# Two banks for the output products of four attention stages, a two-scalar scaling on GpSimd, and the compressed branch moved into the first units

## The reference, cut to what matters

```
o_c = softmax(where(valid_c, q kc^T * scale, NEG_BIG)) * valid_c @ vc      # 31 compressed keys
o_s = softmax(causal(q ks^T * scale)) @ vs
o_w = softmax(causal(q kw^T * scale)) @ vw
o_n = g0 * o_c + g1 * o_s + g2 * o_w
```

## Time and profile before

| | |
|---|---|
| median of 3 runs | 3747.55 (3745.74 to 3749.96) |
| the profiled execution's own time | 3756.65 |
| its span | 3754.8 |
| TensorE busy, share of the span | 3329.8 (89%) |
| VectorE, ScalarE, GpSimd busy | 1294.7, 976.5, 401.7 |
| mean granted TensorE clock | 0.943 |
| stage "at", layer 0 | from 261.2 to about 418 |
| stage "at", layer 1 | from 1148.0 to about 1310 |
| stage "mla" | from 2085.6 to about 2156 |
| stage "gqa" | from 2962.4 to about 3081 |

### The profile page before, as it was taken

How to read it: one execution, slowest core, us unless ns; L and a number is a source line. 1 busy time by engine, 2 the same in 40 slices (tenths; PEclk the granted TensorE clock), 3 DMA queues, 4 the chain that set the end, 5 groups by cost and what they waited for, 6 DMA issues and landing times. The chain is left out here.

```text
span 3754.8 us, 42733 instructions
## 1 busy us (share of the span) xinstructions
PE 3329.8 (89%) x17174; PEld 2288.9 (61%) x17174; DVE 1294.7 (34%) x1709; ACT 976.5 (26%) x1557; POOL 401.7 (11%) x403
## 2 busy tenths in 40 slices
PE   7999899998999899999756769999988787999996
PEld 6875587877876487787644367444436346644442
DVE  4324543333523444242344543111113644311112
ACT  4225333222324414231221431000013343100001
POOL 1005100000104300000000610000000561000000
PEclk9999999999998999999977989999998898999998
DMA  5410223333320014331300123999982101499996
GB/s 154 124 45 1 68 81 99 90 90 80 106 90 23 12 56 135 90 93 42 101 7 14 45 80 120 416 424 424 424 341 80 45 23 58 195 420 424 424 423 289
DMA packets 286517, 587.41 MB, mean 156 GB/s; under 512 B 34666, under 2 KB 228408, under 8 KB 237200
## 3 DMA queue, kind: packets, MB, share of 16 engines
q1 hardware_dynamic: 286352, 585.11, 41.9%
HBM read 581.92 MB, written 2.10 MB: 156 GB/s over the span
## 5 line engine op out<-in xcount | busy, mean ns | idle before, releaser
L2010 PE MATMUL ps<-w_ring,xe 128*64 128x512 f32 x1024 | 232.7, 597 | 6.7 <-PEq L109 5.0
L305 PE MATMUL ps<-h_hi,in_w_hi 128*128 128x512 f32 (+1 forms) x528 | 210.1, 398 | 12.8 <-DVE in_w_lo L353 8.2
L305 PE MATMUL ps<-u_hi,mlp_w_hi 128*128 128x512 f32 x512 | 202.3, 395 | 12.0 <-DVE u_lo L976 12.0
L305 PE MATMUL ps<-h_lo,in_w_hi 128*128 128x512 f32 (+1 forms) x528 | 208.4, 395 | 0.0
L305 PE MATMUL ps<-h_hi,in_w_lo 128*128 128x512 f32 (+1 forms) x528 | 207.8, 394 | 0.0
L353 DVE TENSOR_TENSOR mlp_w_lo<-w_ring,mlp_w_hi 128x2048 fp32r<-128x2048 f32 x64 | 146.7, 2292 | 176.9 <-ACT mlp_w_hi L321 176.9
L305 PE MATMUL ps<-h_hi,mlp_w_hi 128*128 128x512 f32 x512 | 199.3, 389 | 3.0 <-DVE h_lo L367 3.0
L305 PE MATMUL ps<-u_lo,mlp_w_hi 128*128 128x512 f32 x512 | 201.4, 393 | 0.0
L305 PE MATMUL ps<-u_hi,mlp_w_lo 128*128 128x512 f32 x512 | 201.1, 393 | 0.0
L305 PE MATMUL ps<-h_lo,mlp_w_hi 128*128 128x512 f32 x512 | 199.2, 389 | 0.0
L305 PE MATMUL ps<-h_hi,mlp_w_lo 128*128 128x512 f32 x512 | 199.2, 389 | 0.0
(11 more groups left out here) (513 smaller groups left out, 7176.0 us busy)
## 6 DMA issues: line engine op xcount, KB each, us to landing
w_ring<-in_w SPq DMA_DIRECT2D x192, 1024.0 KB, 12.8
ex_front<-in_w SPq DMA_DIRECT2D x96, 1024.0 KB, 13.3
ex_back<-in_w SPq DMA_DIRECT2D x96, 1024.0 KB, 13.5
w_ring<-in_w_in SPq DMA_DIRECT2D x32, 1024.0 KB, 6.4
w_ring<-in_w_up SPq DMA_DIRECT2D x32, 1024.0 KB, 5.8
w_ring<-in_w_down SPq DMA_DIRECT2D x32, 1024.0 KB, 5.7
w_ring<-in_cmp_w SPq DMA_DIRECT2D x16, 512.0 KB, 4.2
w_ring<-in_w_out SPq DMA_DIRECT2D x8, 1024.0 KB, 6.4
```

What stands on the lines that cost most here:

```text
L305: mm = pe.matmul(ps[0:o.rows, k % banks, 0:o.cols], lhsT, rhs, start=(j == 0), stop=(j == len(o.mm) - 1))
L2010: mm = pe.matmul(ps[rows, bank + half, :], lhsT, slot(2 * m + a)[:, kk, 512 * half:512 * half + 512], start=(k == 0), stop=(k == DC - 1))
```

## The change

It has three parts.

1. The output products of successive chunks alternate between banks 6 and 7 (`bank_of`). The first product of a chunk now waits for the `o_done` of the chunk before last.
2. GpSimd scales the probabilities of ungated groups with two scalars, the second a column of ones, in place of one.
3. In "at", only the two mask products stay ahead of the first unit. `cmp_scores` moves to step 2. The VectorE maxima and subtraction follow in step 2, ScalarE's exponential in step 3, VectorE's sums in step 4, GpSimd's multiplication before its unit 4, and `cmp_flip` with its two copies in step 6; it now uses banks 6 and 7 and not T_BANK. The wait for `sel` moves into the first unit, the wait for the copies to the first output product.

```diff
+C_SCORES, C_FLIP = 2, LAG + TT - 1
...
+    def bank_of(g):
+        return O_BANK + (chunks_done[g] - closes(g)) % 2
...
+                    if cmp and u == 0:
+                        pe.wait_ge(s.sel_made, 1)
...
-                    elif cmp:
-                        pe.wait_ge(s.c_copied, 2)
...
-                        if opens and chunks_done[g] - closes(g) > 0:
-
-                            pe.wait_ge(s.o_done, chunks_done[g] - closes(g))
+                        if cmp and g == 0:
+
+                            pe.wait_ge(s.c_copied, 2)
+                        if opens and chunks_done[g] - closes(g) > 1:
+
+                            pe.wait_ge(s.o_done, chunks_done[g] - closes(g) - 1)
...
-                    cmp_scores()
-                    pe.wait_ge(s.sel_made, 1)
+                    cmp_masks()
                 for step in range(nu + LAG + 1 + TT):
+                    if cmp and step == C_SCORES:
+                        cmp_scores()
                     if step < nu:
                         scores(step)
-                    if cmp and step == LAG - 1:
+                    if cmp and step == C_FLIP:
                         cmp_flip()
...
                 for u in range(nu):
+                    if cmp and u == C_SCORES + 2:
+                        pool.wait_ge(s.c_inverse, 1)
...
-                        if groups[g].gate:
-                            ins = pool.tensor_scalar(p, p, inv[:, u % 8, a:a + 1], groups[g].gate(a, i), ALU.mult, ALU.mult)
-                        else:
-                            ins = pool.tensor_scalar(p, p, inv[:, u % 8, a:a + 1], None, ALU.mult)
+                        gate = groups[g].gate(a, i) if groups[g].gate else C.ones[:, 0:1]
+                        ins = pool.tensor_scalar(p, p, inv[:, u % 8, a:a + 1], gate, ALU.mult, ALU.mult)
```

More of the change, by code:

```diff
@@ L706, in keep @@
                         act.wait_ge(s.mixed, mixed_by[g])
-                        act.activation(oT.hi[:, groups[g].chunk, :], ps[:, O_BANK, :], ACT.Copy).then_inc(s.o_hi, 1)
+                        act.activation(oT.hi[:, groups[g].chunk, :], ps[:, bank_of(g), :], ACT.Copy).then_inc(s.o_hi, 1)
                 for step in range(nu + LAG + 2 + TT):
-                    if cmp and step == 0:
+                    if cmp and step == C_SCORES + 1:
                         act.wait_ge(s.c_less, 1)
@@ L716, in _ @@
                         exponentials(step)
-                    if cmp and step == LAG - 1:
+                    if cmp and step == C_FLIP:
                         act.wait_ge(s.c_flipped, 1)
-                        act.activation(pcT[:, 0, :], ps[:, T_BANK, :], ACT.Copy).then_inc(s.c_copied, 1)
+                        act.activation(pcT[:, 0, :], ps[:, 6, :], ACT.Copy).then_inc(s.c_copied, 1)
                     if 0 <= step - LAG < nu:
@@ L771, in keep @@
                         dve.wait_ge(s.o_hi, chunks_done[g])
-                        dve.tensor_tensor(oT.lo[:, c, :], ps[:, O_BANK, :], oT.hi[:, c, :].bitcast(F32), ALU.subtract).then_inc(s.o_done, 1)
+                        dve.tensor_tensor(oT.lo[:, c, :], ps[:, bank_of(g), :], oT.hi[:, c, :].bitcast(F32), ALU.subtract).then_inc(s.o_done, 1)
                 v = pc[:, :, :, :, :].rearrange("p a i r n -> p (a i r) n") if cmp else None
@@ L777, in _ @@
                                           C.ident[:, LO:LO + H1].unsqueeze(2).broadcast_to([P, H1, P]), ALU.add).then_inc(s.sel_made, 1)
+                    u = step - LAG - 2 - (TT - 1)
+                    if u >= 0 and u % TT == TT - 1:
+                        keep(u // TT)
+                    if step < nu:
+                        peaks(step)
+                    if 1 <= step <= nu:
+                        inverses(step - 1)
+                    if cmp and step == C_SCORES:
                         dve.wait_ge(s.c_scored, 1)
@@ L782, in _ @@
                         dve.tensor_tensor(v, c_ps, c_small[:, 0, :].unsqueeze(2).broadcast_to([P, 32, 32]), ALU.subtract).then_inc(s.c_less, 1)
-                    u = step - LAG - 2 - (TT - 1)
-                    if u >= 0 and u % TT == TT - 1:
-                        keep(u // TT)
-                    if step < nu:
-                        peaks(step)
-                    if cmp and step == 1:
+                    if cmp and step == C_SCORES + 2:
                         dve.wait_ge(s.c_exped, 1)
@@ L797, in _ @@
                         ins.then_inc(s.c_inverse, 1)
-                    if 1 <= step <= nu:
-                        inverses(step - 1)
-                    if cmp and step == LAG - 1:
+                    if cmp and step == C_FLIP:
                         dve.wait_ge(s.c_flipped, 2)
-                        dve.tensor_copy(pcT[:, 1, :], ps[:, T_BANK + 1, :]).then_inc(s.c_copied, 1)
+                        dve.tensor_copy(pcT[:, 1, :], ps[:, 7, :]).then_inc(s.c_copied, 1)
                     if 0 <= step - LAG < nu:
```

18 lines of the change are left out of this document (8 added, 10 removed).

## The result

The changed kernel takes 3711.44 us (median of 4 runs, 3706.27 to 3716.81). The kernel before, measured in the same session, takes 3748.09. The difference of the medians is 36.65 us where 28.3 were forecast. The ratio on record is 0.9891 with a 95% interval of 0.9874 to 0.9908. In all measurements here this ratio is not the plain quotient of the two medians (0.9902 in this one), so it should be read with its interval. 3711.4 lies inside the forecast range (3706 to 3735), on its fast side. The profiled execution took 3716.81 us with a span of 3715.0 and a mean granted clock of 0.947; before, the span was 3754.8 and the clock 0.943. One run of a later kernel, `split_012`, took 4390.28 us at a granted clock of 0.728: it is in that kernel's median (without it 3709.09), but not in its ratio.

A forecast was written before the change was run, and what follows sets the result against it. TensorE was taken to be held at chunk openings by the output bank's wait, with clock falls behind them. Gains of 16.3 + 0.6 + 5.4 + 6.0 = 28.3 us took the median 3747.55 to 3719.2 us, range 3706 to 3735.

The forecast's parts named there:

- What bounds the stages: Four attention stages: TensorE stops at chunk openings for the output bank; GpSimd's equally long 3.09 us "gqa" round isn't the bound.
- Part 1: Chunk openings: two output banks remove TensorE's wait, 10.4 us in "at", 4.6 in "gqa", 1.3 in "mla", 16.3 in all.
- The lower bound of half: Two output banks: gain of only 8 us if earlier openings merely lead to waits for exponentials two units later.
- Part 2: GpSimd scaling with two scalars: mostly cover, saving 0.6 us where flips wait for GpSimd alone; bounds 0 and 3.
- The walk through layer 1: Start of "at", layer 1, traced engine by engine: first output product at 1176.6 instead of 1179.06, 2.4 us earlier.
- Part 3: Compressed branch moved at the starts of "at": 2.4 us in layer 1, 3.0 in layer 0, 5.4 in all; bounds 0 and 8.
- I take the middle: Start of "at", layer 0: 3.0 us, between 1.8 (clock falls at the same time) and 4.2 (full units keep it up).
- The rival of a branch stretched over units without room: "at", steps 2 to 4: VectorE's extra 4.6 us gives back half the openings' gain; 15 us, 3733; chance 0.12.
- Part 4: Clock falls behind openings vanish once the idle goes: 6 us taken, between 1.8 and 10.9, since the profiled execution exceeded the median.
- The clock that still falls behind the 32-row products: Sparse openings of "at": clock still falls though the idle is gone; gain 22.3 us, 3725; chance 0.25.
- the one that falls behind all eight: Sparse openings: denser narrow work makes the clock fall behind all eight, 37 us lost instead of 10.9; 3751; chance 0.03.
- GpSimd as the pace of "gqa": "gqa" rounds: GpSimd sets the 3.09 us, hiding shape changes that could be shorter; 16 us more, 3703; chance 0.04.

The follow-up runs named there:

- split_012: The changed kernel with the 64 narrow products issued in three pieces, in steps 0, 1 and 2: 3713.83 us, ratio 0.9881.
- scalars_only: The kernel before with only the two-scalar scaling on GpSimd: 3753.49 us, ratio 0.9999.
- banks_only: The kernel before with only the two alternating output banks and their wait: 3722.78 us, ratio 0.9913.
- one_scalar: The changed kernel with GpSimd's one-scalar scaling of before, keeping the two banks and the moved branch: 3726.91 us, ratio 0.9937.
- after_again: The changed kernel run once more, with nothing changed, in a later session: 3713.8 us, ratio 0.9892.
- branch_only: The kernel before with only the compressed branch moved (one output bank, one scalar): 3737.2 us, ratio 0.9965.
- old_wait: The changed kernel, banks still alternating, but waiting for the split of the chunk just before: 3737.11 us, ratio 0.9948.
- scores_1: The changed kernel with the narrow products in step 1 instead of step 2: 3721.91 us, ratio 0.992.
- scores_3: The changed kernel with the narrow products in step 3 instead of step 2: 3729.51 us, ratio 0.9934.
- old_wait_no_pieces: The changed kernel with the old wait at openings and without the 32-row products, leaving out the compressed attention's share of the output: 3724.87 us, single run.

## Why the prediction held, and where its steps were off

**What bounds the stages** held in the main. TensorE's round of 3.09 us in "gqa" is there with GpSimd at half its work (`scalars_only`). The prediction was wrong, though, that 0.17 us is the only idle on the load side: the round also has 0.76 and 0.81 us there, the latter put down to GpSimd's product in the kernel before. It is 0.81 us in `scalars_only` too, now without GpSimd as its releaser, and the matmuls show no idle beside it in either kernel, so it held nothing up. And the openings did wait for the bank and for nothing else.

**Part 1**: 16.3 us forecast, 17.6 measured between the profiles. By stage 10.4, 4.6 and 1.3 were forecast and 11.2, 4.9 and 1.5 found. The "at" part was counted by its waits, and there each opening gives some 0.07 us more than its wait. An opening in "gqa" was said to shorten by 0.67 and shortened by 0.71. The lower bound of half, for later waits on exponentials, did not come up: no such wait stands in the openings. By the case in the Trainium skill ("TensorE: Matmul & The Clock Gate", HAM oscillation) in which double-buffering gave no further gain, this part would have been 0; `banks_only` gave 29.7 us with the clock's share, so the case does not carry over to banks that TensorE is seen to wait for.

**Part 2**: 0.6 us forecast, and alone it is within its bounds of 0 and 3 (ratio 0.9999). In "mla" and "gqa" it gave 0.9 where 0.6 was said. What was mis-sized is the share that was put inside part 3, "a similar 0.6 per layer": `one_scalar` shows 2.08 us in layer 0, and 3.7 in layer 1 against a start with the same clock. The walk through layer 1 took GpSimd as free when the branch's sums were ready, which is true with two scalars and false with one.

**Part 3**: 5.4 us forecast, 2.5 measured between the two profiles: 2.7 in layer 1 against 2.4, and nothing (-0.2) in layer 0 against 3.0. The step that failed is the choice in layer 0 between a clock that falls at the same time (1.8) and one that two full units keep up (4.2), "I take the middle". It was neither: the clock fell 0.9 us after the first product, at 261.4 and not at 265.2, and the narrow products took 7.04 us. The walk in layer 1 was good in its result (28.6 said, 28.36 found) and in its last wait (0.4 said, 0.38 found). Since the start depends on when the clock falls, single profiles are poor evidence, so here is the time to the first output product in all profiles of the four arrangements, sorted by the time from the start of the stage to the clock's fall:

| | narrow products first, fall within 1.2 us | the same, fall at 3.0 to 4.0 us | step 2, fall within 1.2 us | step 2, fall at 6.2 to 7.3 us |
|---|---|---|---|---|
| one scalar | 31.03, 31.37, 31.34 | 28.17, 29.36, 28.14 | 30.43, 30.44 | 27.67, 27.69 |
| two scalars | 31.00, 31.01 | none | 28.35, 28.36, 28.38, 28.35, 28.36, 28.35 | 23.96, 24.95 |

With a fall within 1.2 us, parts 2 and 3 together give 2.7 to 3.0 us a layer, 5.4 to 6 in both, where 5.4 were forecast; part 3 with one scalar gives only 0.6 to 0.9. In the pair of profiles layer 0 compares a late fall before (28.17) with an early one after (28.35), and that hides half of it. Which of the two a layer gets is luck. The rival of a branch stretched over units without room did not happen with step 2, and does happen with 1 and 3.

**Part 4**, the clock, was mis-sized: 6 us were taken, 12.4 measured. Two things are in that. The falls behind openings were worth 10.8 in the profile, as read (10.9), but a fall at the end of "gqa" (5.30 against 3.65 us for 16 products) was not seen at all, though it stood in the timeline. No 32-row product is near it, only 2.0 us of idle. It is the most regular fall of all: the 16 products take 5.25 to 5.35 us in all six profiles with the old wait, and 3.65, behind an idle of 1.36, in all eight without it. So the theory that a fall wants both the idle and the product holds for idles under a microsecond at most. The larger error was the discount from 10.9 to 6, made because the profiled execution was 9.1 us above the median of three runs. The executions of the kernel before in later sessions answer it: 19 runs in one range from 3743.48 to 3758.64 around a median of 3752.45, so the profiled one with 3756.65 is an ordinary one. Their mean granted clocks are 0.940 to 0.947, and 0.941 to 0.944 in the seven runs of the session of `after_again`, around the profile's 0.943. So plain runs lose about as much to the clock as the profiled one; the three runs that I had were on the fast side.

For the profiled execution the sum was 33.2 and the stages gave 33.8. That it comes out so close is in part luck: the openings (+1.3) and the clock (+1.5) make up for the starts (6.0 said, parts 2 and 3, 3.7 found). In the medians the discount of the clock shows: without it the sum would have been 33.2 and not 28.3, nearer to the 36.65 measured. The span was to be 3721.6 and is 3715.0, and 6.0 of that difference are outside the four stages.

**The rivals.** The clock that still falls behind the 32-row products (0.25) and the one that falls behind all eight (0.03) are both refuted by 0 of 64. (The chances of the forecast and the first three rivals add up to 0.92, not 0.91.) GpSimd as the pace of "gqa" is refuted by `scalars_only`, and the Trainium skill's rule ("TensorEngine Tiling (Array Packing)", Key Properties), that a change of tiling mode drains TensorE, agrees with the 0.17 us that stand unchanged in its rows. What stays open: why `branch_only` and `old_wait` lose the clock less often than the kernel before with nearly the same openings, what sets the time of the fall at the start of "at", what makes the falls at the ends of layers, and why `one_scalar` is slower in the median than its stages say.

## What to carry to other kernels

Where a product opens an accumulation and waits for the bank's last reader, alternating two banks can pay even if each wait is under a microsecond: here over a third of the gain came from clock falls that went with the waits, and they are seen only in windows of the clock behind each opening, not in the list of waits. Before an engine that is busy all through a stage is called its bound, look for the round of the engine that it feeds; if the two are equal, halving one can give nothing, as in "gqa". And work that was pure cover can become the path when another part of the change moves a dependent instruction behind it in the same queue, so cost such parts together.

## What the runs showed of the hardware

- GpSimd's product of 128x512 values with one scalar takes 1566 ns and with two scalars, the second a column of ones, 775 ns (and 772 in the changed kernel). The form with more arithmetic is the fast one.
- An idle of 0.80 to 0.91 us followed by 1.07 us of 32-row products cost the granted clock in 10 of 32 cases, an idle of 0.80 us without these products in 0 of 16, the products without idle in 0 of 64. An idle of 2.0 us ahead of the last 16 products of "gqa" cost it in 6 of 6, one of 1.36 us in 0 of 8. Idles of 2.35 to 2.77 us at the starts of "at" (`scores_1`, `scores_3`, `one_scalar`, `branch_only`) were followed or cut by a fall in 6 of 8.
- The 64 narrow products (64 rows, 32 columns each) take 3.76 us when the clock is at its higher level to their end (`old_wait_no_pieces`, layer 1), 4.04 to 4.22 when it falls during the last of them, and 7.04 us at the lower level.
- One program, executed twice, differed by 4.4 us in one stage start (28.36 and 23.96) by the time at which the clock fell.
